# Order of weight loads, place of the gate columns and of the norm turns, and one-tile openings in a two-model kernel

## The reference, cut to what matters

```
for l in range(DEPTH):
    sh_m, sc_m, gt_m, sh_f, sc_f, gt_f = split(silu(c) @ w_ada[l] + b_ada[l])
    h = rms_norm(x, g_pre_mix[l]) * (1 + sc_m) + sh_m
    x = x + gt_m * rms_norm(token_mixer(h, ...), g_post_mix[l])
    h = rms_norm(x, g_pre_ffn[l]) * (1 + sc_f) + sh_f
    x = x + gt_f * rms_norm(conv_glu_ffn(h, ...), g_post_ffn[l])
```

## Time and profile before

| | |
|---|---|
| median of 3 runs | 2782.87 us (2778.92 to 2784.71) |
| the profiled execution's own time | 2781.0 us |
| its span, first to last instruction | 2779.2 us |
| PE busy | 2501.5 us, 90% |
| PE weight loads busy | 2088.4 us, 75% |
| DVE busy | 1726.5 us, 62% |
| ACT busy | 1080.9 us, 39% |
| POOL busy | 443.0 us, 16% |
| mean granted clock of TensorE | 0.960 |
| mean rate of the transfers | 149 GB/s |

### The profile page before, as it was taken

How to read it: one execution, slowest core, us unless ns; L and a number is a source line. 1 busy time by engine, 2 the same in 40 slices (tenths; PEclk the granted TensorE clock), 3 DMA queues, 4 the chain that set the end, 5 groups by cost and what they waited for, 6 DMA issues and landing times. The chain is left out here.

```text
span 2779.2 us, 34851 instructions
## 1 busy us (share of the span) xinstructions
PE 2501.5 (90%) x13320; PEld 2088.4 (75%) x13320; DVE 1726.5 (62%) x2571; ACT 1080.9 (39%) x1818; POOL 443.0 (16%) x471
## 2 busy tenths in 40 slices
PE   4886879797988799999797999999999998999898
PEld 3675777676986787887664888888888887777898
DVE  6966667775888577677496556445555456344454
ACT  3444434354545322224575432223322224233543
POOL 1100010100111112111493112111012111000011
PEclk9997999897999999999899999999999999999999
DMA  7634557461556345354110234333333434321462
GB/s 293 213 129 168 203 212 285 148 222 46 198 208 234 134 177 194 139 195 166 40 61 26 69 140 153 121 145 124 113 132 133 149 131 159 99 83 62 144 197 99
DMA packets 118293, 413.00 MB, mean 149 GB/s; under 512 B 13552, under 2 KB 17776, under 8 KB 118128
## 3 DMA queue, kind: packets, MB, share of 16 engines
q1 hardware_dynamic: 117568, 409.06, 41.8%
q10 hardware_dynamic: 560, 1.72, 0.2%
HBM read 409.68 MB, written 1.05 MB: 148 GB/s over the span
## 5 line engine op out<-in xcount | busy, mean ns | idle before, releaser
L1057 PE MATMUL ps<-hH,sh 128*128 128x256 f32 (+1 forms) x2560 | 854.2, 334 | 107.4 <-DVE sl L1618 78.6
L1328 ACT ACTIVATE sh<-raw 128x1024 fp32r<-128x1024 f32 x534 | 551.0, 1043 | 933.6 <-DMA raw<-in_w 669.0
L1058 PE MATMUL ps<-hL,sh 128*128 128x256 f32 (+1 forms) x2560 | 845.7, 330 | 0.0
L1059 PE MATMUL ps<-hH,sl 128*128 128x256 f32 (+1 forms) x2560 | 844.8, 330 | 0.0
L1618 DVE TENSOR_TENSOR sl<-raw,sh 128x1024 fp32r<-128x1024 f32 x534 | 655.3, 1252 | 146.2 <-ACT sh L1328 145.1
L1057 PEld LDWEIGHTS ps<-hH,sh 128*128 128x128 f32 x2560 | 492.2, 192 | 164.7 <-issue 74.9
L1631 DVE CUSTOM_DVE_ANT_0 mjunk<-raw,cB,V 128x1024 bf16<-128x1024 f32 x384 | 522.7, 1361 | 26.3 <-DMA C<-in_cst 8.4
L1058 PEld LDWEIGHTS ps<-hL,sh 128*128 128x128 f32 x2560 | 491.6, 192 | 48.9 <-issue 1.2
L1059 PEld LDWEIGHTS ps<-hH,sl 128*128 128x128 f32 x2560 | 491.1, 192 | 48.5
L1057 PE MATMUL ps<-sh,uHh 128*128 128x512 f32 x792 | 314.7, 397 | 22.3 <-DVE sl L1618 22.2
L2110 POOL TENSOR_TENSOR uLl<-F,uHh 128x256 fp32r<-128x256 f32 (+1 forms) x132 | 154.4, 1170 | 1106.8 <-ACT uHh L1508 937.2
(11 more groups left out here) (168 smaller groups left out, 2180.2 us busy)
## 6 DMA issues: line engine op xcount, KB each, us to landing
raw<-in_w SPq DMA_DIRECT2D x756, 512.0 KB, 4.4
raw<-in_w SPq DMA_DIRECT2D x16, 256.0 KB, 3.8
cB<-in_rpb SPq DMA_DIRECT2D x64, 64.0 KB, 2.8
X<-in_x ACTq DMA_DIRECT2D x1, 1024.0 KB, 11.8
X<-in_ctx SPq DMA_DIRECT2D x1, 1024.0 KB, 8.3
out<-X SPq DMA_DIRECT2D x2, 512.0 KB, 2.6
raw<-in_w SPq DMA_DIRECT2D x2, 288.0 KB, 6.1
cB<-in_c ACTq DMA_DIRECT2D x1, 512.0 KB, 5.5
```

What stands on the lines that cost most here:

```text
L1057: self.e.matmul(out, lh, rh, start=start, stop=False)
L1058: self.e.matmul(out, lh, rl, start=False, stop=False)
L1059: return self.e.matmul(out, ll, rh, start=False, stop=stop)
L1328: self.e.activation(self.m["sh"][k % SPL][:, 0:w], self.m["raw"][n % RAW][:, 0:w], ACT.Copy).then_inc(self.sems["w_hi"], 1)
```

## The change

1. `finish` writes a list `loads`: split units where their `upper` stands, modulation units where their `mod` step stands. SP issues by position `r` in that list, and the raw buffer and its semaphore go by `r` too.
2. `ffn1` puts eight empty entries in `aside` ahead of its gate, `ffn2` five.
3. `products` runs the waiting `firsts` and `seconds` behind the unit `at` of its first pass (3 of 0 to 5, or 2 of 0 to 3), and no longer between the passes.
4. `ffn1` and the two-tile `ffn2` open with `products` over four units, 128 columns (one tile) a pass.
5. Where a stage ends on two tiles, tile 0's `firsts` and `seconds` run ahead of the gate work of tile 1's last half, not within it.
6. `na` runs six query products ahead of the values (parts run after 0 and 3), and two in the attention rounds.

```diff
@@ down
+                if i and len(tiles) == 2:
+                    self.first_parts()
+                    self.second_parts()
                 done(t, half, banks[i])
@@ products
-                if not second and len(self.firsts) > 1 and j == 0:
-                    self.firsts.pop(0)()
+                if not second and (j == at or j == 0 and len(self.firsts) > 1):
+                    self.first_parts(0 if j == at else 1)
                     self.second_parts()
-            if not second:
-                self.finish_norms()
@@ mixer, output product
-                    if i == 1 and kp == 2 and half == 0:
-                        self.first_parts(1)
-                        self.second_parts()
+                if half:
+                    self.first_parts()
+                    self.second_parts()
                 self.gate_half(i, half, banks[half][i], gid, AB, hid, st2)
@@ ffn1
-        self.finish_norms()
         self.rate = RATES[f"up{l}"]
+        head = self.products([(n, l, c * 128) for c in range(2) for n in ("w_up_act", "w_up_lin")],
+                             (slice(0, 128), slice(128, 256)), ("h", hid), 2)
+        self.aside += [lambda: None] * 8
         gid = self.gates_later("w_ada", l, 5, ("g_post_ffn", (l,)), 1)
@@ ffn2
+        head = self.products([(n, (l, half_i), c * 128) for c in range(3 if n4 else 2) for n in
+                              ("ffn_w_gate_2", "ffn_w_up_2")],
+                             cols if n4 else (slice(0, 128), slice(128, 256)), ("h", hid), 3 if n4 else 2)
+        self.aside += [lambda: None] * 5
@@ na
-        for c in range(4):
+        for c in range(6):
             part(0, c)
-            if c == 1:
-                self.first_parts(1)
+            if c in (0, 3):
+                self.first_parts(1 if c == 0 else 0)
                 self.second_parts()
-        self.finish_norms()
-            if c + 4 < KD:
-                part(0, c + 4)
+            if c in (1, 3):
+                part(0, 6 + c // 2)
@@ finish
+                        loads.append(n)          # with each upper
+                loads.append(s["unit"])          # with each mod
+        self.loads = loads
+        self.load_no = {n: k for k, n in enumerate(loads)}
@@ Sync.issue (and likewise the readers of a raw buffer)
-        if n >= RAW:
-            self.wait_ge(self.got("raw_left", n - RAW))
+        if r >= RAW:
+            self.wait_ge(self.got("raw_left", r - RAW))
+        n = self.plan.loads[r]
```

More of the change, by code:

```diff
@@ L293, in product, with products @@
         return b
-    def products(self, specs, cols, act):
+    def products(self, specs, cols, act, at=3):
         got = []
@@ L550, in ffn1 @@
         for c in range(KF):
[L551 to L554, removed]
+            if head:
+                ba, bu = head.pop(0), head.pop(0)
+                if late:
+                    late.pop(0)()
+            else:
+                ba = self.product("w_up_act", l, c * 128, slice(0, 256), ("h", hid))
+                if late:
+                    late.pop(0)()
+                bu = self.product("w_up_lin", l, c * 128, slice(0, 256), ("h", hid))
             if late:
@@ L580, in ffn2 @@
     def ffn2(self, l, half_i, tiles, hid, ab_next, cols=(slice(0, 256), slice(256, 512)), done2=None):
[L581 to L585, removed]
-            self.finish_norms()
+        n4 = len(tiles) == 4
+        head = self.products([(n, (l, half_i), c * 128) for c in range(3 if n4 else 2) for n in
+                              ("ffn_w_gate_2", "ffn_w_up_2")],
+                             cols if n4 else (slice(0, 128), slice(128, 256)), ("h", hid), 3 if n4 else 2)
         ns = len(tiles) // 2
@@ L849, in finish @@
     def finish(self):
-        out, n, ctx, top, used, order, lower = [], 0, False, 0, set(), [], []
+        out, n, ctx, top, used, order, lower, loads = [], 0, False, 0, set(), [], [], []
         for s in self.steps:
@@ L1000, in issue @@
     def issue(self):
-        n = self.next
-        if n >= len(self.plan.units):
+        r = self.next
+        if r >= len(self.plan.loads):
             return
         self.next += 1
-        if n >= RAW:
-            self.wait_ge(self.got("raw_left", n - RAW))
+        if r >= RAW:
+            self.wait_ge(self.got("raw_left", r - RAW))
+        n = self.plan.loads[r]
         _, w, _ = self.plan.kinds[n]
         src = bass.AP(tensor=self.dram["w"].tensor, offset=self.plan.units[n][2], ap=[[w, P], [1, w]])
-        self.e.dma_start(self.m["raw"][n % RAW][:, 0:w], src).then_inc(self.sems[f"raw{n % RAW}"], 16)
+        self.e.dma_start(self.m["raw"][r % RAW][:, 0:w], src).then_inc(self.sems[f"raw{r % RAW}"], 16)
     def load(self, s):
@@ L1107, in prod @@
         w = cols.stop - cols.start
-        out = self.buf(b)[:, cols] if w == 256 and "begun" in s else self.buf(b)[:, 0:w]
+        out = self.buf(b)[:, cols] if "begun" in s else self.buf(b)[:, 0:w]
         for k in range(KD):
@@ L1323, in upper @@
         n, w = s["n"], s["w"]
-        k = self.plan.split_no[n]
-        self.e.wait_ge(self.sems[f"raw{n % RAW}"], 16 * (n // RAW + 1))
+        k, r = self.plan.split_no[n], self.plan.load_no[n]
+        self.e.wait_ge(self.sems[f"raw{r % RAW}"], 16 * (r // RAW + 1))
         if k >= SPL:
             self.wait_ge(self.got("w_used", self.plan.split_unit[k - SPL]))
-        self.e.activation(self.m["sh"][k % SPL][:, 0:w], self.m["raw"][n % RAW][:, 0:w], ACT.Copy).then_inc(
+        self.e.activation(self.m["sh"][k % SPL][:, 0:w], self.m["raw"][r % RAW][:, 0:w], ACT.Copy).then_inc(
             self.sems["w_hi"], 1)
@@ L1613, in lower @@
         n, w = s["n"], s["w"]
-        k = self.plan.split_no[n]
-        hi, lo, raw = self.m["sh"][k % SPL], self.m["sl"][k % SPL], self.m["raw"][n % RAW]
-        self.e.wait_ge(self.sems[f"raw{n % RAW}"], 16 * (n // RAW + 1))
+        k, r = self.plan.split_no[n], self.plan.load_no[n]
+        hi, lo, raw = self.m["sh"][k % SPL], self.m["sl"][k % SPL], self.m["raw"][r % RAW]
+        self.e.wait_ge(self.sems[f"raw{r % RAW}"], 16 * (r // RAW + 1))
         self.wait_ge(self.got("w_hi", n))
@@ L1619, in lower @@
             self.sems["w_lo"], 1)
-        self.done("w_lo", ("w_lo", n), ("raw_left", n))
+        self.done("w_lo", ("w_lo", n), ("raw_left", r))
     def mod(self, s):
@@ L1624, in mod @@
         ns = 1 if name == "w_ada" else 2
-        raw = self.m["raw"][n % RAW]
-        self.e.wait_ge(self.sems[f"raw{n % RAW}"], 16 * (n // RAW + 1))
+        r = self.plan.load_no[n]
+        raw = self.m["raw"][r % RAW]
+        self.e.wait_ge(self.sems[f"raw{r % RAW}"], 16 * (r // RAW + 1))
         self.wait_ge(self.got("c_act" if ns == 1 else "ctx_act"))
@@ L1632, in mod @@
                                         scalar=o, op0=ALU.mult, op1=ALU.add, accum_out=o).then_inc(self.sems["v_mod"], 1)
-            self.done("v_mod", ("mod", name, l, u, st), *([("raw_left", n)] if st == ns - 1 else []))
+            self.done("v_mod", ("mod", name, l, u, st), *([("raw_left", r)] if st == ns - 1 else []))
     def coef(self, s):
```

## The result

The changed kernel takes 2749.40 us (median of 4 runs, 2746.47 to 2765.1) against 2782.16 for the kernel before (4 runs, 2778.92 to 2784.71): a ratio of 0.9894, 95% interval 0.9856 to 0.9933. The forecast was 2715.5 and its range 2685 to 2747. The sign was right; the gain is 33 us where 67 were forecast, and the time lies above the range. The profiled execution took 2749.53 us, its span 2747.7.

What follows compares the result with a forecast made beforehand. The prediction took PE, busy 90% of the span, as the bound, with up loops held back by load refill order. Gains less prices summed to 67.4 us, 2781.0 to 2713.6, or 2715.5 on the median's scale; range 2685 to 2747.

Steps and rivals of the forecast that it cites:

- two tiles opened with one: Up-stage and last-stage openings: 128-column matmuls at 0.112 us; gain 8.5 us at layer 0, loss 4.8 in each other.
- loads: Loads in order of use: gains of 33 and 16 us in up loops, 3 and 5 in down stages, 4.5 later.
- layer 0: burst gone: Layer 0's head: forced modulation units and PE's 12.78 us idle time vanish, counted within the opening's 8.5 us gain.
- late conditioning vectors: Layer 1's up stage: last w_ada unit comes about one turn before the new vectors' first use; 3 us lost.
- mixer sums: Second mixer: five more modulation sums, 1.3 us each on DVE beside chains, costing 2 us.
- burst and turns: First four-tile half: one unit less in the burst gains 3 us; norm turns inside first passes gain 13.
- attention entry: Neighbourhood attention: six modulation units fill the window, delaying both query products behind the burst; 11.5 us lost.
- A: Rival, chance 0.13: up loops open only half because DVE sets their pace; half the loads' 62.5 us goes, 2746.
- B: Rival, chance 0.10: loops open wholly and stalls elsewhere go too; 28 us better, 2688.
- C: Rival, chance 0.04: buffers were not the limit, load order changes nothing; 2778, within noise.
- D: Rival, chance 0.04: more loads in flight land more slowly, lengthening each up-loop turn; slower at 2812.
- E: Rival, chance 0.03: one-tile matmuls in the openings go at 0.081 us; 18 us off, 2698.

Runs made afterwards that it cites:

- run 3: The changed kernel plus fourteen unused 256-column float32 matmuls in PE's idle time ahead of the last stage's opening; 2727.64 us, ratio 0.98.
- run 2: The changed kernel, but both layers' ffn1 and the two-tile ffn2 open with both tiles at once (256 columns); 2714.10 us, ratio 0.9746.
- run 1: The kernel before with only the load order changed (loads and raw buffers by order of use); 2708.51 us, ratio 0.9732.
- run 8: The changed kernel without the empty entries, so the gates' columns are forced as early as before; 2738.96 us, ratio 0.9835.
- run 10: The kernel before with load order, norm turns inside first passes, later layer-0 gates, rates leaving nothing for attention, and six query products moved; no one-tile openings; 2686.04 us.
- run 5: The changed kernel with the last stage's one-tile opening over six product units instead of four; 2765.01 us, ratio 0.9896.
- run 6: The changed kernel with rate late 0.6 for 0.5, so no modulation units are left for neighbourhood attention; 2734.87 us, ratio 0.9817.

## Why the prediction was wrong

The step that failed is "two tiles opened with one". It took 0.112 us for a 128-column matmul, from a stretch at 72 columns, and allowed "2 for the slower clock behind the gap". The 0.112 is right at 2.4 GHz (run 3). But that stretch was not one that began behind a gap; these openings do, and there the spacing is 0.213, for 72 to 181 matmuls. The cost is 0.101 us each: some 7.4 us in each of layers 0 and 1, and in the last stage 18.3 (181 narrow ones) and 1.8 more for the 18 wide ones behind them. The 2 us were the price of a 256-column opening, which leaves the low clock after 21 to 27 matmuls (run 2). My bounds of 2 better and 3 worse did not hold it, since nothing in them doubled a price. The page of the Trainium skill that the prediction weighed, TensorE: Matmul & The Clock Gate, gives two clock levels in its section What's actually happening, with the lower one after an idle time. The trace agrees: 0.50 behind the 3.30 us gap of layer 0. The forecast took up only the section on spacing and put the clock at 2 us. Whichever spacing had been chosen, 0.081 or 0.112, the error would have stayed.

The steps of the prediction, from stage starts in the profiled executions of before, after, runs 1 and 2 (us, plus is a gain). Where no run is named, the figures go from run 1 to run 2; in the two rows marked *, from run 1 to the kernel after:

| step | forecast | measured | from |
|---|---|---|---|
| loads (with layer 1's own 3 apart) | 65.5 | 74.7 | before to run 1 |
| layer 0: burst gone | with the opening 8.5 | 9.0 | run 1 to run 2, end of the up stage |
| layer 0: opening | | -10.0 | run 2 to after |
| late conditioning vectors | -3 | -5.5 | layer 1's up stage, 126.0 to 131.5 |
| mixer entry | 3.5 | 3.6 | 70.5 to 66.9 |
| mixer sums | -2 | -5.3 | 193.5 to 198.8 |
| burst and turns * | 3 + 13 | 14.2 | 9.7 up to the last half, 4.5 for the turn in it |
| layer 1's down stage * | 0 | -2.7 | 66.1 to 68.8 |
| attention entry | -11.5 | -14.7 | last half and attention, 641.3 to 651.5, with 4.5 of its turn added |
| opening, layer 1 | -4.8 | -10.6 | run 2 to after |
| opening, last stage | -4.8 | -20.4 | run 2 to after |
| last stage otherwise | 0 | -0.8 | 194.2 to 195.0 |
| sum | 67.4 | 31.5 | span: 31.5 |

Of the 35.9 us that are missing, layer 0's head and the other two openings account for 30.9. All other steps fell 14.2 short together, and the loads came out 9.2 above.

- *Loads.* Right in mechanism, some 9 us too small. By stage: layer 0's up 39.5 (33 forecast), downs 7.8 and 8.4 (3 and 5), layer 1's up 19.7 (19 without the vectors). The 4.5 beyond 1060 us did not come at all (-0.8): those four waits are not of this kind, run 1 still has them. The period fell to PE's own time as said.
- *Gates later.* The count of units by hand was exact, six left at the attention. All three prices were somewhat too low, within their bounds but for the attention (5 to 13, measured 14.7): each part of the bill that was "DVE beside chains" came out dearer. Run 8, which differs in nothing else from the kernel after, gets back 1.8 us in the mixer, 6.6 in layer 1's up stage and 6.9 at the attention and loses 14.5 in layer 0's up stage; at the start of the last stage it is 2.8 ahead, of which 1.1 was there before layer 0's up stage began. So the part gave nothing net, and about half of the 14.7 at the attention is not of its making. That this half comes from the query products' new place beside the burst is argued only: without the burst their move costs nothing (run 10).
- *Openings.* The early starts were right (10.0 and 9.3 us earlier, 7 forecast). The price was 20.6 and 29.7, not 12.
- *Turns.* Three of four went, the convolution's did not: its PE was about to wait for its vectors anyway.
- *Rivals.* A is refuted by run 1, though its 2746 lies near the result: a near number for the wrong reason. B came true for the loops alone. C and D fell with SP's waits and 286 GB/s. E is refuted: 0.112 at 2.4 GHz.
- *Range.* The bounds given for the two up loops are 17 and 11 us worse, 28 together and not 22. Added straight to the 12 for the prices they reach 2755.5, so the upper end of 2747 was tighter than the terms behind it. That sum would have held the measured time, but by waits in the loops, which did not come.

Of the signs of failure named ahead, "if 128 columns cost more than 256" pointed at the right place, but did not come true as it stands: at the same clock they cost the same per matmul (0.112 against 0.114 to 0.118, and 0.213 both), so two passes cost twice. What failed was the level of the clock, for which no sign was named.

What stays open: why the clock rises behind tile 1's transpositions in some executions and not in others, and what the executions that were not profiled did (2738.42 us in run 5, 2744.18 in run 6).

## What to carry to other kernels

Refill a ring of buffers in the order in which it is drained, and look at who releases the loading queue: that alone gave 2.7% here. When an edit splits wide matmuls into narrow ones behind an idle gap, allow for the low clock over their whole length, and read the clock column beside the busy column, since a stretch at half clock shows as work and not as a wait. Deferred work lands where the plan collects it: count what arrives there, and set the rates so that nothing does.

## What the runs showed of the hardware

- Pairs of a weight load and a 128-column matmul stand 0.112 us apart at a granted clock of 1.00 and 0.213 at 0.50; 256-column ones 0.114 to 0.118 and 0.213. Half the columns saved 0.002 to 0.006 us at 1.00 and nothing at 0.50.
- PE busy without a break did not bring the clock back: 43.0 us in the last stage of the kernel after, 65.0 in run 5. It was back 4.1 and 3.9 us behind the first 256-column matmul. Openings with 256 columns from the start (run 2) were at 1.00 after 4.6 to 5.9 us.
- Fourteen float32 matmuls of 256 columns (28 rows, 6.21 us) in the idle time in front of the opening kept it at 1.00 and gained 22 us.
- One unchanged program ran at 2738.42 and 2765.51 us on one chip (run 5), with mean granted clocks of 0.961 and 0.951; such a spread is itself a sign to look at the clock of each stage.
